# Five networks, five addresses for their rounded weights

## The chip, the cores and the metric

The kernel runs on one core of a Trainium2 chip. The metric is the time of one execution on the device in microseconds (us), the median of several runs. The profile is one further execution, recorded by the hardware profiler; its span goes from the first to the last instruction.

## The reference

Two transformer blocks are computed on 256 positions of width 1024, all in float32. In outline:

```
h = x;  h = h + mixer(rms_norm(h)) @ w_out
h = h + swiglu(rms_norm(h), w_gate, w_up, w_down)        # network 0; then rms_norm
for layer in 0, 1:
    x = x + 0.5 * swiglu(rms_norm(x), ffn_w_in[layer, 0], ffn_w_out[layer, 0])   # networks 1 and 3
    x = x + mixer_layer(rms_norm(x))
    x = x + 0.5 * swiglu(rms_norm(x), ffn_w_in[layer, 1], ffn_w_out[layer, 1])   # networks 2 and 4
swiglu(u) = (silu(u @ w_gate) * (u @ w_up)) @ w_down     # 1024 -> 2816 -> 1024
```

There are five such feed-forward networks ("ffn"), all of one size. Three mixers (attention of several kinds and two recurrences) lie between them, each with a projection in and one out.

## The kernel before

All weights come in through a ring of four slots of 128 x 3072 float32, loaded by SyncE's queue in the order of use. A network is worked off in 22 chunks of 128 of its 2816 inner columns; one chunk fills one slot: 1024 columns of gate, 1024 of up, 1024 of down.

The matrix products are done in a rounded float32 type (fp32r) that TensorE takes in one pass, and precision is regained by splitting each operand into a rounded part and the rounded rest. Each product is three passes, `PASSES = [(0, 0), (1, 0), (0, 1)]`: rounded weights by rounded activations, rest of the weights by rounded activations, rounded weights by the rest of the activations. For each chunk of a network

- ScalarE rounds gate and up into `w_gu[:, j, 0]` (`hi_a`, 2048 columns) and down into `w_dn[:, j, 0]` (`hi_b`, 1024 columns), where j is the chunk's parity;
- VectorE subtracts and leaves the rest in `w_gu[:, j, 1]` (`lo_a`) and `w_dn[:, j, 1]` (`lo_b`);
- TensorE does gate and up (`gate_up`): for each of 2 matrices, 8 pieces k and 3 passes, it loads 128 columns of `w_gu` as the stationary operand (a weight load, PEld) and streams 256 columns of the activations `uT_h` or `uT_l` past them (a matmul): 48 matmuls of 256 columns;
- ScalarE and VectorE make silu(gate) * up from the result and split it into `h_r`;
- TensorE does down (`down`) of the chunk before: here the activations `h_r` are stationary, 128 columns each, and 512 columns of `w_dn` are streamed: 12 matmuls of 512 columns.

TensorE loads the stationary operand of the next matmul while the present one streams. In a name such as `ps<-uT_h,w_gu` the streamed operand stands first, the stationary second, and in `ps<-w_dn,h_r` it is `w_dn` that is streamed.

The middle 16 chunks are a loop on each engine, the other six are written out; addresses repeat with the parity. The projections outside the networks use the same three passes with other buffers: `in_h`, `even_h`, `odd_h` for the rounded weights, `out_h` for those of the projections out, and `ring_r`, the ring itself, for the rest of their weights. Small sets of columns have `gate_w` (24 columns) and `odd_small` (8 columns).

Where things lie matters here, so the addresses are worked out from the sizes. Tensors are laid one after another. `x`, `xn`, `uT`, `yT` (whose space `uT_l` uses), `inh` (`in_h`), `gate_r`, `ring` and `ffb` (`h_r`) all have sizes that are multiples of 256 bytes, so all of them begin at the same address modulo 256. Then comes `cst` with 4662 float32, 18,648 bytes, which takes 18,656 with the next tensor at a multiple of 32; that is 224 modulo 256. `msk` (2304 bytes) and `small` (1024) keep it. So `wk`, the large work area that holds `w_gu`, `w_dn`, `even_h`, `odd_h` and `out_h`, begins 224 bytes past the activations modulo 256. Called phase below: (address of the weights minus address of the activations) modulo 256. Pieces within a tensor are 512 bytes apart for 128 columns and 1024 for 256, so the phase is the same for every matmul of a network: 224. In `in_h` and `ring_r` it is 0; in `even_h` and `out_h` it is 224. The slices of `gate_w` are 96 bytes apart and those of `odd_small` 32, so they go through many phases.

Of the kernel before, what the change touches and what calls it, by code (L numbers as in the profile page):

```python
# [7 lines left out]
F32 = mybir.dt.float32  # L8
# [7 lines left out]
P = 128  # L16
T, D = 256, 1024
TT, KC = T // P, D // P
F = 2816
FC = F // P  # L20
# [31 lines left out]


MASKS = 512 + 2 * LEVELS * P


IN_ITEMS = ([("col", 0), ("col", 1)] + [("col", b) for b in range(2, 6)] + [("zw", j) for j in range(4)]
# [38 lines left out]
def build(nc, x_in, wstream, gains, consts_in, masks_in, scratch, tri, inv, out):  # L96
    ctx = ExitStack()
    with ctx:
# [6 lines left out]
        def over(name, shape, under, skip=0):  # L105

            return nc.alloc_sbuf_tensor_at(name, shape, F32R, offset=at[under] + 4 * skip)
# [12 lines left out]
        s = {n: ctx.enter_context(nc.semaphore(n)) for n in names}  # L120
# [10 lines left out]
        cst = sb("cst", [P, NCONST])  # L131
        msk = sb("msk", [P, MASKS], U8)
        small = sb("small", [P, 256])
        WK = 20480
        wk = sb("wk", [P, WK])
        ps = [ctx.enter_context(nc.psum_tensor(f"ps{i}", [P, 512], F32)) for i in range(8)]
# [13 lines left out]

        ident = C("ident")

        w_gu = over("w_gu", [P, 2, 2, 2 * D], "wk")
        w_dn = over("w_dn", [P, 2, 2, D], "wk", 8 * D)
        h_r = over("h_r", [P, 2, 2, T], "ffb")
        ring_r = over("ring_r", [P, RING, SLOT], "ring")

# [5 lines left out]
        w_small = [over(f"even_small{i}", [P, KC * 40], "wk", 14336 + KC * 40 * i) for i in range(2)]  # L163
        wo_h = [over(f"out_h{i}", [P, SLOT], "wk", o) for i, o in enumerate((13312, 17408, 10240))]
        uT_r = [over("uT_h", [P, KC, T], "uT"), over("uT_l", [P, KC, T], "yT")]
        sg = wk[:, 12 * D:12 * D + 2 * T].rearrange("p (a b) -> p a b", a=2)
        ss = [small[:, 0:1], small[:, 1:2], small[:, 8:9]]
        ss3 = [small[:, 242:243], small[:, 243:244]]
        ss4 = [small[:, c:c + 1] for c in (0, 245, 1, 8)]
# [48 lines left out]
        mu_rest, k_a_rest = small[:, 224:238], small[:, 238:242]  # L218
        spread_heads = W(10240 + MASKS, P)

# [17 lines left out]
        MT_AT, n = {}, 0  # L238
# [140 lines left out]
        IB, n = {}, 0  # L379
# [51 lines left out]
        def _(sp):  # L431
# [3 lines left out]
            for i in range(RING):  # L435
# [5 lines left out]
                if i == 1:  # L441
                    sp.dma_start(cst[:, FIRST:NCONST], consts_in[:, FIRST:NCONST]).then_inc(s["consts_loaded"], 16)
            sp.dma_start(W(10240, MASKS + P), masks_in).then_inc(s["masks_loaded"], 16)
            rounds = (NSLOTS - RING) // RING
# [43 lines left out]
        def slot(i):  # L488
            return ring[:, i % RING, :]
# [3 lines left out]
        def _(pe):  # L493
# [3 lines left out]
            def mm(o, l, r, start=True, stop=True):  # L497
                return pe.matmul(o, l, r, start=start, stop=stop, skip_group_check=True)  # L498
# [49 lines left out]

            PASSES = [(0, 0), (1, 0), (0, 1)]

            def gate_up(j, between=None):
                for m in range(2):
                    if m and between:
                        between()
                    for k in range(KC):
                        for n, (a, b) in enumerate(PASSES):
                            w = w_gu[:, j % 2, a, (m * KC + k) * P:(m * KC + k + 1) * P]
                            last = mm(ps[4 + 2 * m + j % 2][:, 0:T], w, uT_r[b][:, k, :],
                                      k == 0 and n == 0, k == KC - 1 and n == 2)
                    last.then_inc(s[("gu_gate", "gu_ps")[m]], 1)  # L560

            def first_gate_up(norm):

                for k in range(KC):
                    pe.wait_ge(s["uT_hi"], 16 * TN[norm] + 8 + k + 1)
                    for m in range(2):
                        for a in range(2):
                            mm(ps[4 + 2 * m][:, 0:T], w_gu[:, 0, a, (m * KC + k) * P:(m * KC + k + 1) * P],
                               uT_r[0][:, k, :], k == 0 and a == 0, False)
                for m in range(2):  # L570
                    for k in range(KC):
                        if not m:
                            pe.wait_ge(s["uT_lo"], 16 * TN[norm] + 8 + k + 1)
                        last = mm(ps[4 + 2 * m][:, 0:T], w_gu[:, 0, 0, (m * KC + k) * P:(m * KC + k + 1) * P],
                                  uT_r[1][:, k, :], False, k == KC - 1)
                    last.then_inc(s[("gu_gate", "gu_ps")[m]], 1)

            def spread_rstd(norm):

                pe.wait_ge(s["diag_ready"], 2 * TN[norm] + 2)  # L580
                for t in range(TT):
                    last = mm(ps[0][:, t * P:(t + 1) * P], C("ones"), diag[:, t, :])
                last.then_inc(s["bc_ps"], 1)
                if norm == 1:
                    mm(ps[1][0:16, 0:384], C("t5")[0:32, :], C("t5_onehot")[0:32, :]).then_inc(s["t5_ps"], 1)

            def down_part(j, t, half, start, stop):
                for n, (a, b) in enumerate(PASSES):
                    last = mm(ps[2 * t + half][:, :], h_r[:, j % 2, a, t * P:(t + 1) * P],
                              w_dn[:, j % 2, b, half * 512:(half + 1) * 512], start and n == 0, stop and n == 2)  # L590
                return last

            def down(j, start):
                for t, half in PARTS:
                    last = down_part(j, t, half, start, False)
                last.then_inc(s["down_done"], 1)

            def ffn(f, norm):
                q = FC * f

                def step(c, r=0):

                    pe.wait_ge(s["lo_a"], r + (q + c + 1))
                    if q + c >= 2:
                        pe.wait_ge(s["h_ready"], r + (q + c - 1))
                    if c == 0:
                        first_gate_up(norm)
                    else:
                        gate_up(c, (lambda: spread_rstd(norm)) if c == 1 else None)
                    if 0 < c < FC - 1:  # L610
                        pe.wait_ge(s["lo_b"], r + (q + c))
                        pe.wait_ge(s["h_ready"], r + (q + c))
                        if norm == 1 and c == 1:
                            pe.wait_ge(s["t5_sb"], 1)
                        down(c - 1, c == 1)
                step(0)
                step(1)
                with pe.Fori(0, 4 * LOOPS, 4) as r:
                    for j in range(4):
                        step(2 + j, r)  # L620
                for c in range(2 + 4 * LOOPS, FC):
                    step(c)

                n = NORM_AFTER_FFN[f]
                pe.wait_ge(s["lo_b"], q + FC - 1)
                pe.wait_ge(s["h_ready"], q + FC - 1)
                for t, half in PARTS[0:3]:
                    down_part(FC - 2, t, half, False, False)
                pe.wait_ge(s["lo_b"], q + FC)
                pe.wait_ge(s["h_ready"], q + FC)  # L630
                for t, half in PARTS[0:3]:
                    down_part(FC - 1, t, half, False, True).then_inc(s["acc_done"], 1)
                first_T(n, 0)
                down_part(FC - 2, 1, 1, False, False).then_inc(s["down_done"], 1)
                down_part(FC - 1, 1, 1, False, True).then_inc(s["down_done"], 1)
                first_T(n, 1)

            def piece(o, j):
# [647 lines left out]
        def _(act):  # L1286
# [75 lines left out]
            def hi_a(f, c, r=0, rr=0):  # L1362

                q, i = FC * f, BASE[f"ffn{f}"] + c
                act.wait_ge(s[f"land{i % RING}"], rr + 16 * (i // RING + 1))
                if q + c >= 2:
                    act.wait_ge(s["gu_ps"], r + (q + c - 1))
                act.copy(w_gu[:, c % 2, 0, :], slot(i)[:, 0:2 * D]).then_inc(s["hi_a"], 1)  # L1368

            def hi_b(f, c, r=0):  # L1370
                q, i = FC * f, BASE[f"ffn{f}"] + c
                if q + c >= 2:
                    act.wait_ge(s["down_done"], r + (q + c - 1))
                act.copy(w_dn[:, c % 2, 0, :], slot(i)[:, 2 * D:3 * D]).then_inc(s["hi_b"], 1)  # L1374

            def ffn(f, norm):
                q = FC * f
# [585 lines left out]
        def _(v):  # L1963
# [60 lines left out]
            def lo_a(f, c, r=0):  # L2024

                q, i = FC * f, BASE[f"ffn{f}"] + c
                v.wait_ge(s["hi_a"], r + (q + c + 1))
                v.tensor_tensor(w_gu[:, c % 2, 1, :], slot(i)[:, 0:2 * D], w_gu[:, c % 2, 0, :].bitcast(F32),  # L2028
                                ALU.subtract).then_inc(s["lo_a"], 1)

            def lo_b(f, c, r=0):
                q, i = FC * f, BASE[f"ffn{f}"] + c
                v.wait_ge(s["hi_b"], r + (q + c + 1))
                v.tensor_tensor(w_dn[:, c % 2, 1, :], slot(i)[:, 2 * D:3 * D], w_dn[:, c % 2, 0, :].bitcast(F32),  # L2034
                                ALU.subtract).then_inc(s["lo_b"], 1)
                v.wait_ge(s["lo_b"], r + (q + c + 1))
                v.sem_inc(s[f"free{i % RING}"], 1)
# [762 lines left out]
```

## Time and profile before

| | |
|---|---|
| time, median of 3 runs | 1424.88 us (1424.19 to 1425.08) |
| span of the profiled execution | 1422.4 us |
| what lies around the span (median less span) | 2.5 us |
| TensorE matmul busy | 1395.2 us, 98% |
| VectorE busy | 944.7 us, 66% |
| ScalarE busy | 691.0 us, 49% |
| mean granted TensorE clock | 0.999 |

The profile gives the span only of the profiled execution, not a time of its own on the scale of the runs, so the difference between the median and the span stands in the table in its place. The busy time of one matmul in the profile contains its way through the array (some 0.28 us for 256 columns) and overlaps with the next one's. What a matmul costs in a row of many is the distance from one start to the next, and that is read from the timeline: take the starts of two rows and divide by the number of matmuls between them.

### The profile page before, as it was taken

The numbers are of one execution on the slowest core, as the hardware profiler recorded it, in microseconds if no ns is written. First come the engines' busy times: TensorE is split into PE (matmuls) and PEld (weight loads), VectorE is DVE, ScalarE is ACT, GpSimd is POOL, SyncE is SP. The second block draws the span as 40 slices with busy tenths as digits, with TensorE's granted clock in tenths as the row PEclk, the third lists the DMA queues.
The fourth block names the chain that finished last, engine by engine and source line by source line (L and its number), as shares of the span: only waits on it lengthen the run. The fifth ranks groups of instructions, "written<-read, shape, count | busy, mean of one in ns | idle before, by whom it ended". The sixth has DMA issues, their size and how long they took to land. (4 is left out here: it accounts for less than half of the span.)

```text
span 1422.4 us, 25483 instructions
## 1 busy us (share of the span) xinstructions
PE 1395.2 (98%) x10044; PEld 1286.2 (90%) x10044; DVE 944.7 (66%) x1539; ACT 691.0 (49%) x1107; POOL 82.9 (6%) x137
## 2 busy tenths in 40 slices
PE   8999999999999999999999999999999999999997
PEld 8898888999989999899989999999998988899997
DVE  5778567766668666567577666676665676676665
ACT  6764545433454443376654433444433655643342
POOL 1030010000020000000000000100000123000000
PEclk9999999999999999999999999999999999999999
DMA  9344005645526555433356545365554423465540
GB/s 359 135 160 185 2 25 228 222 177 183 197 108 228 209 184 177 178 104 133 120 207 224 189 177 182 129 229 198 194 177 178 149 90 134 177 222 180 194 158 30
DMA packets 33069, 239.47 MB, mean 168 GB/s; under 512 B 6864, under 2 KB 13280, under 8 KB 14304
## 3 DMA queue, kind: packets, MB, share of 16 engines
q1 hardware_dynamic: 30320, 234.84, 45.6%
q10 hardware_dynamic: 2672, 3.58, 0.7%
q8 instruction: 51, 0.84, 0.2%
q14 instruction: 26, 0.21, 0.0%
HBM read 236.15 MB, written 2.25 MB: 168 GB/s over the span
## 5 line engine op out<-in xcount | busy, mean ns | idle before, releaser
L498 PE MATMUL ps<-uT_h,w_gu 128*128 128x256 f32 x3520 | 614.1, 279 | 2.5 <-ACT uT_h L1316 2.5
L498 PEld LDWEIGHTS ps<-uT_h,w_gu 128*128 128x128 f32 x3520 | 538.0, 188 | 13.8 <-issue 5.0
L498 PE MATMUL ps<-uT_l,w_gu 128*128 128x256 f32 x1760 | 478.8, 279 | 0.0
L498 PE MATMUL ps<-w_dn,h_r 128*128 128x512 f32 x1320 | 325.7, 396 | 0.3 <-DVE h_r L2070 0.3
L498 PEld LDWEIGHTS ps<-uT_l,w_gu 128*128 128x128 f32 x1760 | 325.5, 188 | 0.0
L498 PEld LDWEIGHTS ps<-w_dn,h_r 128*128 128x128 f32 x1320 | 239.6, 188 | 51.3 <-issue 1.4
L1368 ACT CAST w_gu<-ring 128x2048 fp32r<-128x2048 f32 x110 | 210.0, 1909 | 156.2 <-PE ps L498 155.6
L2028 DVE TENSOR_TENSOR w_gu<-ring,w_gu 128x2048 fp32r<-128x2048 f32 x110 | 252.1, 2292 | 35.2 <-ACT w_gu L1368 35.2
L2061 DVE TENSOR_TENSOR us<-ps,bc 128x256 f32<-128x256 f32 x110 | 46.5, 423 | 203.2 <-PE ps L498 203.2
L1381 ACT ACTIVATE wk<-wk 128x256 f32<-128x256 f32 x110 | 46.1, 419 | 260.7 <-DVE wk L2059 260.7
L1374 ACT CAST w_dn<-ring 128x1024 fp32r<-128x1024 f32 x110 | 115.7, 1052 | 82.8 <-PE ps L498 82.7
L2034 DVE TENSOR_TENSOR w_dn<-ring,w_dn 128x1024 fp32r<-128x1024 f32 x110 | 134.1, 1219 | 5.3 <-ACT w_dn L1374 5.1
L498 PE MATMUL ps<-uT_h,ring_r 128*128 128x256 f32 x408 | 114.4, 281 | 0.0
L498 PE MATMUL ps<-wk 128*128 128x64 f32 (+6 forms) x504 | 76.9, 303 | 1.9 <-DVE small L2337 0.7
L498 PEld LDWEIGHTS ps<-uT_h,ring_r 128*128 128x128 f32 x408 | 77.5, 190 | 0.6 <-issue 0.2
L2059 DVE TENSOR_TENSOR wk<-ps,bc 128x256 f32<-128x256 f32 x110 | 46.7, 425 | 35.8 <-PE ps L498 22.0
L498 PEld LDWEIGHTS ps<-wk 128*128 128x128 f32 (+3 forms) x504 | 56.1, 186 | 7.4 <-issue 2.0
L498 PE MATMUL ps<-ring_r,uT_h 128*128 128x512 f32 (+2 forms) x176 | 62.0, 353 | 0.0
L2064 DVE TENSOR_TENSOR wk<-wk,us 128x256 f32<-128x256 f32 x110 | 46.7, 425 | 7.7 <-ACT wk L1381 4.3
L498 PE MATMUL ps<-uT_h,in_h 128*128 128x256 f32 x176 | 50.5, 289 | 1.0 <-DVE ring_r L2021 1.0
L2070 DVE TENSOR_TENSOR h_r<-wk,h_r 128x256 fp32r<-128x256 f32 x110 | 46.8, 425 | 3.7
L498 PE MATMUL ps<-uT_l,in_h 128*128 128x256 f32 x176 | 48.7, 283 | 0.0
(398 smaller groups left out, 1696.0 us busy)
## 6 DMA issues: line engine op xcount, KB each, us to landing
ring<-wstream SPq DMA_DIRECT2D x144, 1536.0 KB, 6.6
cst<-consts_in SPq DMA_DIRECT2D x1, 2185.0 KB, 13.7
wk<-t_row ACTq DMA_DIRECT2D x1, 2048.0 KB, 8.0
wk<-masks_in SPq DMA_DIRECT2D x1, 1216.0 KB, 24.1
x<-x_in SPq DMA_DIRECT2D x2, 512.0 KB, 4.7
ring<-wstream SPq DMA_DIRECT2D x1, 1024.0 KB, 8.8
inh<-gains ACTq DMA_DIRECT2D x2, 512.0 KB, 9.6
tri_blocks<-wk SPq DMA_DIRECT2D x3, 256.0 KB, 2.8
```

Of the source, the lines that this page charges most:

```text
L498: return pe.matmul(o, l, r, start=start, stop=stop, skip_group_check=True)
L1368: act.copy(w_gu[:, c % 2, 0, :], slot(i)[:, 0:2 * D]).then_inc(s["hi_a"], 1)
L1374: act.copy(w_dn[:, c % 2, 0, :], slot(i)[:, 2 * D:3 * D]).then_inc(s["hi_b"], 1)
L1381: act.activation(sg[:, c % 2, :], sg[:, c % 2, :], ACT.Silu).then_inc(s["silu_ready"], 1)
L2028: v.tensor_tensor(w_gu[:, c % 2, 1, :], slot(i)[:, 0:2 * D], w_gu[:, c % 2, 0, :].bitcast(F32), ALU.subtract).then_inc(s["lo_a"], 1)
L2034: v.tensor_tensor(w_dn[:, c % 2, 1, :], slot(i)[:, 2 * D:3 * D], w_dn[:, c % 2, 0, :].bitcast(F32), ALU.subtract).then_inc(s["lo_b"], 1)
L2059: v.tensor_tensor(h, ps[4 + c % 2][:, 0:T], bc[:], ALU.mult).then_inc(s["gs_ready"], 1)
L2061: v.tensor_tensor(us[:], ps[6 + c % 2][:, 0:T], bc[:], ALU.mult).then_inc(s["us_ready"], 1)
L2064: v.tensor_tensor(h, h, us[:], ALU.mult).then_inc(s["h_mul"], 1)
L2070: v.tensor_tensor(hr[:, 1, :], h, hr[:, 0, :].bitcast(F32), ALU.subtract).then_inc(s["h_ready"], 1)
```

## The change

`w_gu` and `w_dn`, one tensor each for all networks, become separate tensors for each network and parity. Network f begins FFN_AT[f] elements into `wk`, which is 64, 128, 192, 224 and 96 bytes; with the 224 of `wk` the phases are 32, 96, 160, 192 and 64. The buffers of the two parities are set apart by P = 128 elements (512 bytes), so that two networks' buffers of different parity do not overlap where one network's first chunks are rounded while the last one is being finished. `sg`, which holds the gate's result, moves 2048 bytes on. Nothing else changes: each instruction is there as before, in its order, with its waits.

```
+FFN_AT = [16, 32, 48, 56, 24]
...
-        w_gu = over("w_gu", [P, 2, 2, 2 * D], "wk")
-        w_dn = over("w_dn", [P, 2, 2, D], "wk", 8 * D)
+        w_gu = [[over(f"w_gu{2 * f + j}", [P, 2, 2 * D], "wk", FFN_AT[f] + j * (4 * D + P)) for j in range(2)]
+                for f in range(5)]
+        w_dn = [[over(f"w_dn{2 * f + j}", [P, 2, D], "wk", FFN_AT[f] + 2 * (4 * D + P) + j * (2 * D + P))
+                 for j in range(2)] for f in range(5)]
...
-        sg = wk[:, 12 * D:12 * D + 2 * T].rearrange("p (a b) -> p a b", a=2)
+        sg = wk[:, 12 * D + 4 * P:12 * D + 4 * P + 2 * T].rearrange("p (a b) -> p a b", a=2)
...
-                            w = w_gu[:, j % 2, a, (m * KC + k) * P:(m * KC + k + 1) * P]
+                            w = w_gu[f][j % 2][:, a, (m * KC + k) * P:(m * KC + k + 1) * P]
...
-                              w_dn[:, j % 2, b, half * 512:(half + 1) * 512], start and n == 0, stop and n == 2)
+                              w_dn[f][j % 2][:, b, half * 512:(half + 1) * 512], start and n == 0, stop and n == 2)
...
-                act.copy(w_gu[:, c % 2, 0, :], slot(i)[:, 0:2 * D]).then_inc(s["hi_a"], 1)
+                act.copy(w_gu[f][c % 2][:, 0, :], slot(i)[:, 0:2 * D]).then_inc(s["hi_a"], 1)
...
-                v.tensor_tensor(w_gu[:, c % 2, 1, :], slot(i)[:, 0:2 * D], w_gu[:, c % 2, 0, :].bitcast(F32),
+                v.tensor_tensor(w_gu[f][c % 2][:, 1, :], slot(i)[:, 0:2 * D], w_gu[f][c % 2][:, 0, :].bitcast(F32),
                                 ALU.subtract).then_inc(s["lo_a"], 1)
```

`hi_b`, `lo_b` and `first_gate_up` are changed in the same way.

## Rows read from the trace of the kernel before

**Rows 1.** The page: busy time, share and instructions; TensorE's clock in 40 slices
```profile
PE 1395.2 (98%) x10044; PEld 1286.2 (90%) x10044; DVE 944.7 (66%) x1539; ACT 691.0 (49%) x1107; POOL 82.9 (6%) x137
...
PEclk9999999999999999999999999999999999999999
```

**Rows 2.** Windows over networks 0 and 1, 2 and 3, and 4
```profile
226.00:601.80 375.80, 374.11 (x2666) 348.26 (x2666) 251.49 (x353) 161.35 (x177) 11.82 (x17) 1.00 0.54 194
726.60:1100.30 373.70, 373.15 (x2664) 348.09 (x2664) 247.97 (x347) 157.50 (x170) 5.48 (x9) 1.00 0.54 192
1229.20:1414.60 185.40, 185.40 (x1323) 173.17 (x1324) 120.39 (x170) 76.45 (x79) 1.49 (x4) 1.00 0.45 166
```

**Rows 3.** Groups on the page: forms, count, busy us, mean ns, idle before
```profile
L498 PE MATMUL ps<-uT_h,w_gu 128*128 128x256 f32 x3520 | 614.1, 279 | 2.5 <-ACT uT_h L1316 2.5
...
L498 PE MATMUL ps<-uT_l,w_gu 128*128 128x256 f32 x1760 | 478.8, 279 | 0.0
L498 PE MATMUL ps<-w_dn,h_r 128*128 128x512 f32 x1320 | 325.7, 396 | 0.3 <-DVE h_r L2070 0.3
```

**Rows 4.** Timeline, PE, network 0: two chunks in the loop
```profile
325.55 0.40 PE L498 MATMUL ps<-uT_h,w_gu 128*128 128x256 f32 x2
...
331.15 2.96 PE L498 MATMUL ps<-w_dn,h_r 128*128 128x512 f32 x12
333.95 0.40 PE L498 MATMUL ps<-uT_h,w_gu 128*128 128x256 f32 x2
```

**Rows 5.** Timeline, PE, projection in: phase 0; 12 matmuls between the first two rows
```profile
25.06 0.28 PE L498 MATMUL ps<-uT_h,ring_r 128*128 128x256 f32 x1
...
26.50 0.28 PE L498 MATMUL ps<-uT_h,ring_r 128*128 128x256 f32 x1
...
31.90 0.28 PE L498 MATMUL ps<-uT_h,ring_r 128*128 128x256 f32 x1
```

**Rows 6.** Timeline, PE, even projection, weights stationary: 54 matmuls between
```profile
614.22 0.28 PE L498 MATMUL ps<-uT_h,even_h 128*128 128x256 f32 x1
...
620.58 0.28 PE L498 MATMUL ps<-uT_h,even_h 128*128 128x256 f32 x1
```

**Rows 7.** Timeline, PE, even projection, weights streamed: 30 matmuls between
```profile
624.66 0.28 PE L498 MATMUL ps<-even_h,uT_h 128*128 128x256 f32 x1
...
628.19 0.28 PE L498 MATMUL ps<-even_h,uT_h 128*128 128x256 f32 x1
```

**Rows 8.** Timeline, PE, projection out, 512 columns streamed: 21 matmuls between
```profile
214.75 0.39 PE L498 MATMUL ps<-ring_r,uT_h 128*128 128x512 f32 x1
...
219.65 0.39 PE L498 MATMUL ps<-ring_r,uT_h 128*128 128x512 f32 x1
```

**Rows 9.** Timeline, PE, 24 stationary columns at many phases: 18 matmuls between
```profile
91.98 0.39 PE L498 MATMUL ps<-uT_h,gate_w 128*24 128x256 f32 x2
...
94.03 0.40 PE L498 MATMUL ps<-uT_h,gate_w 128*24 128x256 f32 x2
```

**Rows 10.** Timeline, PE, 8 stationary columns at many phases: 18 matmuls between
```profile
1109.23 0.39 PE L498 MATMUL ps<-uT_h,odd_small 128*8 128x256 f32 x2
...
1111.33 0.39 PE L498 MATMUL ps<-uT_h,odd_small 128*8 128x256 f32 x2
```

**Rows 11.** Groups, ACT and DVE, by form: rounding and subtracting at two phases
```profile
L1374 ACT CAST w_dn<-ring 128x1024 fp32r<-128x1024 f32 x110 | 115.7, 1052 | 82.8 <-PE ps L498 82.7
...
L1354 ACT CAST in_h<-ring 128x1024 fp32r<-128x1024 f32 x24 | 25.2, 1059 | 0.9 <-DMA ring<-wstream 0.3
...
L2034 DVE TENSOR_TENSOR w_dn<-ring,w_dn 128x1024 fp32r<-128x1024 f32 x110 | 134.1, 1219 | 5.3 <-ACT w_dn L1374 5.1
...
L2021 DVE TENSOR_TENSOR ring_r<-ring,in_h 128x1024 fp32r<-128x1024 f32 x24 | 31.0, 1296 | 12.2 <-ACT in_h L1354 11.5 <-DVE wk L2109 0.5
```

**Rows 12.** Timeline, DVE, network 0: the work of one chunk
```profile
331.35 0.42 DVE L2061 TENSOR_TENSOR us<-ps,bc 128x256 f32<-128x256 f32 x1 [2.37 <-PE ps L498]
...
332.59 0.42 DVE L2070 TENSOR_TENSOR h_r<-wk,h_r 128x256 fp32r<-128x256 f32 x1
333.35 2.29 DVE L2028 TENSOR_TENSOR w_gu<-ring,w_gu 128x2048 fp32r<-128x2048 f32 x1 [0.33 <-ACT w_gu L1368]
```

More of the change, by code:

```diff
@@ L549, in _, with gate_up @@
             PASSES = [(0, 0), (1, 0), (0, 1)]
-            def gate_up(j, between=None):
+            def gate_up(f, j, between=None):
                 for m in range(2):
@@ L560, in gate_up, with first_gate_up @@
                     last.then_inc(s[("gu_gate", "gu_ps")[m]], 1)
-            def first_gate_up(norm):
+            def first_gate_up(f, norm):
                 for k in range(KC):
@@ L567, in first_gate_up @@
                         for a in range(2):
-                            mm(ps[4 + 2 * m][:, 0:T], w_gu[:, 0, a, (m * KC + k) * P:(m * KC + k + 1) * P],
+                            mm(ps[4 + 2 * m][:, 0:T], w_gu[f][0][:, a, (m * KC + k) * P:(m * KC + k + 1) * P],
                                uT_r[0][:, k, :], k == 0 and a == 0, False)
@@ L573, in first_gate_up @@
                             pe.wait_ge(s["uT_lo"], 16 * TN[norm] + 8 + k + 1)
-                        last = mm(ps[4 + 2 * m][:, 0:T], w_gu[:, 0, 0, (m * KC + k) * P:(m * KC + k + 1) * P],
+                        last = mm(ps[4 + 2 * m][:, 0:T], w_gu[f][0][:, 0, (m * KC + k) * P:(m * KC + k + 1) * P],
                                   uT_r[1][:, k, :], False, k == KC - 1)
@@ L585, in spread_rstd, with down_part, down @@
                     mm(ps[1][0:16, 0:384], C("t5")[0:32, :], C("t5_onehot")[0:32, :]).then_inc(s["t5_ps"], 1)
-            def down_part(j, t, half, start, stop):
+            def down_part(f, j, t, half, start, stop):
                 for n, (a, b) in enumerate(PASSES):
                     last = mm(ps[2 * t + half][:, :], h_r[:, j % 2, a, t * P:(t + 1) * P],
-                              w_dn[:, j % 2, b, half * 512:(half + 1) * 512], start and n == 0, stop and n == 2)
+                              w_dn[f][j % 2][:, b, half * 512:(half + 1) * 512], start and n == 0, stop and n == 2)
                 return last
-            def down(j, start):
+            def down(f, j, start):
                 for t, half in PARTS:
-                    last = down_part(j, t, half, start, False)
+                    last = down_part(f, j, t, half, start, False)
                 last.then_inc(s["down_done"], 1)
@@ L606, in step @@
                     if c == 0:
-                        first_gate_up(norm)
+                        first_gate_up(f, norm)
                     else:
-                        gate_up(c, (lambda: spread_rstd(norm)) if c == 1 else None)
+                        gate_up(f, c, (lambda: spread_rstd(norm)) if c == 1 else None)
                     if 0 < c < FC - 1:
@@ L614, in step @@
                             pe.wait_ge(s["t5_sb"], 1)
-                        down(c - 1, c == 1)
+                        down(f, c - 1, c == 1)
                 step(0)
@@ L627, in ffn @@
                 for t, half in PARTS[0:3]:
-                    down_part(FC - 2, t, half, False, False)
+                    down_part(f, FC - 2, t, half, False, False)
                 pe.wait_ge(s["lo_b"], q + FC)
@@ L631, in ffn @@
                 for t, half in PARTS[0:3]:
-                    down_part(FC - 1, t, half, False, True).then_inc(s["acc_done"], 1)
+                    down_part(f, FC - 1, t, half, False, True).then_inc(s["acc_done"], 1)
                 first_T(n, 0)
-                down_part(FC - 2, 1, 1, False, False).then_inc(s["down_done"], 1)
-                down_part(FC - 1, 1, 1, False, True).then_inc(s["down_done"], 1)
+                down_part(f, FC - 2, 1, 1, False, False).then_inc(s["down_done"], 1)
+                down_part(f, FC - 1, 1, 1, False, True).then_inc(s["down_done"], 1)
                 first_T(n, 1)
@@ L1373, in hi_b @@
                     act.wait_ge(s["down_done"], r + (q + c - 1))
-                act.copy(w_dn[:, c % 2, 0, :], slot(i)[:, 2 * D:3 * D]).then_inc(s["hi_b"], 1)
+                act.copy(w_dn[f][c % 2][:, 0, :], slot(i)[:, 2 * D:3 * D]).then_inc(s["hi_b"], 1)
             def ffn(f, norm):
@@ L2033, in lo_b @@
                 v.wait_ge(s["hi_b"], r + (q + c + 1))
-                v.tensor_tensor(w_dn[:, c % 2, 1, :], slot(i)[:, 2 * D:3 * D], w_dn[:, c % 2, 0, :].bitcast(F32),
+                v.tensor_tensor(w_dn[f][c % 2][:, 1, :], slot(i)[:, 2 * D:3 * D], w_dn[f][c % 2][:, 0, :].bitcast(F32),
                                 ALU.subtract).then_inc(s["lo_b"], 1)
```

## The prediction

> **What bounds the kernel.** I read the page first: TensorE is busy 98% of the span at full clock, VectorE 66%, ScalarE 49% [rows 1]. The reader is to see that only TensorE can set the time. Then the windows over the five networks: they last 375.8, 373.7 and 185.4 us, 934.9 of 1422.4 us together, with TensorE busy in 932.7 of them and the granted clock 1.00, its upper level of 2.4 GHz [rows 2]. TensorE waits there for almost nothing: 2.5 and 0.3 us in front of the network's matmuls in all [rows 3]. So the networks cost what their matmuls cost, one after another, and the question is only whether an address changes that.
>
> The mean of one matmul (279 and 396 ns) [rows 3] does not tell, as it contains the way through the array. The starts do. In network 0 a chunk's 48 matmuls of gate and up go from 325.55 to 331.15, 5.60 us, and its 12 of down from there to 333.95, 2.80 us [rows 4]. That is 116.7 ns for 256 streamed columns and 233.3 ns for 512. The bare streaming at 2.4 GHz would be 106.7 and 213.3, so both pay the same 9.4% on top: proportional to the streamed columns, although the 512 have one weight load beside them like the 256. The whole is 5 x 22 x 8.4 = 924 us, which agrees with the windows less their beginnings and ends.
>
> **Does the address matter to TensorE?** The other stages show three things.
> - Where weights and activations have phase 0 throughout, in the projection in, the distance is 120.0 ns: 12 matmuls in 1.44 us, 57 in 6.84 [rows 5]. There every matmul costs 3.3 ns more than in the networks at phase 224, at the same clock.
> - In the even projection two of three operands of the weights lie at 224 and one, `ring_r`, at 0. With the weights stationary 54 matmuls take 6.36 us, 117.8 ns [rows 6]. If the third at phase 0 costs 120.0, the other two cost (3 x 117.8 - 120.0) / 2 = 116.7, the networks' value. Some part of the price goes with the address.
> - With the roles turned (weights streamed, activations stationary) the same mixture takes 3.53 us for 30, 117.7 ns [rows 7]. There the stationary operand lies 224 behind, which is 32 ahead, of the streamed one. So 32 costs what 224 costs, 116.7.
>
> With 512 streamed columns the mixture takes 4.90 us for 21, 233.3 ns [rows 8], exactly down's value: there a third at phase 0 costs nothing that can be seen.
>
> Small stationary operands go through many phases: 24 columns at steps of 96 bytes take 2.05 us for 18, 114 ns [rows 9], and 8 columns at steps of 32 bytes 2.10 us for 18, 116.7 ns [rows 10]. So the least seen is 114, the most 120, and 116.7 comes again and again, in the last case whatever the phase.
>
> **The Trainium skill on this.** The rows say that phase 0 costs 3.3 ns a matmul [rows 4, 5]. The Trainium skill, SBUF — State Buffer, section "Who interferes with whom", gives TensorE two independent read ports, one for the streamed operand and one for the weight load, and counts no contention between them; by it no phase could matter and the change would be worth exactly nothing. The trace does not agree for phase 0. The Trainium skill, TensorE: Matmul & The Clock Gate, section "Back-to-back issue gap", gives N / 2.4 + 2.5 ns, that is 109.2 for 256 and 215.8 for 512; if the new addresses brought that, 5280 x 7.5 + 1320 x 17.5 ns, an estimate of 63 us from that page, would go. No row of 256 or 512 columns in this rounded type reaches it.
>
> **The change part by part.**
> - Network 0, phase 32: 116.7 as before, by the turned mixture. 0 us. Down then has 224 as its own difference, which gate and up have now: 0.
> - Networks 1 and 2, phases 96 and 160, and networks 3 and 4, phases 192 and 64. No row shows 128 stationary columns at these. The bounds for a matmul of 256 are 113.9 and 120.0 [rows 9, 5]. There are 1056 in a network: 1056 x 2.8 = 3.0 us less at one end, 1056 x 3.3 = 3.5 us more at the other. For down (264 matmuls) the rows show no difference between a mixture and the phase 32 alone; in proportion to the columns its bounds are 264 x 5.6 = 1.5 less and 264 x 6.7 = 1.8 more. A network can move by -4.5 to +5.3 us, four of them by -18 to +21.
> - I take 0 for each of them, 116.7 ns. The nearest rows are those of 128 stationary columns at 224 and 32, and the 8 columns, which keep 116.7 through all multiples of 32.
> - Writing the weights: ScalarE's rounding takes 1052 ns at 224 and 1059 at 0; VectorE's subtraction 1219 against 1296, with another layout of the columns too [rows 11]. If all phases cost VectorE 6% on its 2292 and 1219 ns, that is 0.21 us per chunk. It is covered: `h_r` is ready at 332.59 + 0.42 = 333.01 and wanted by the down after the next gate and up, at 333.95 + 5.60 = 339.55; `w_gu` of the chunk after next is ready at 333.35 + 2.29 = 335.64 and wanted at 333.95 + 8.40 = 342.35 [rows 12, 4]. VectorE is busy 251.5 of 375.8 us in the networks 0 and 1 [rows 2]. Without that cover it would be 23 us for 110 chunks.
> - Buffers further apart, `sg` moved by 2048 bytes: no wait is added, nothing is moved past a queue, DMAs are the same. 0.
>
> Sum: 0 on 1422.4 us of span; with the 2.5 around it 1424.9. The median stands exactly there.
>
> **The rivals.**
> 1. *Collisions repeat every 64 bytes* (slower). If the two streams disturb one another when they meet in the same 64 bytes, then 64 and 192 are like 0, and 32, 96, 160 and 224 are one class. For it: 32 and 224 alike; and in the 8 columns the same times come back with every second piece. Against it: the 24 columns meet multiples of 64 as well and stay at 114 in the mean. Networks 3 and 4 then pay 2 x 3.5 = +7.0 us, 2 x 1.8 more if down pays too: 1432 to 1435.5. It decides once either is over 117.0 ns a matmul with nothing gained elsewhere.
> 2. *Distance helps* (faster). 0 costs most, 32 less, and further away it goes on falling to the 114 seen. For it: 120, 116.7 and 114 are all there. Against it: 8 columns at many phases stay at 116.7. With 64 and 192 alone at 114 it is 2 x 3.0 = 6 us, with all four and down 18: 1419 to 1407.
> 3. *Other phases are worse* in a way that no row shows, beyond the class of 64: two or four networks at 120 or so, +7 to +21: 1432 to 1446.
> 4. *The address is not the cause*: the projection in is slow for its banks or its code, and nothing changes. Same time as my forecast, and no network differs from another; I count it with it.
>
> **How the numbers follow.** A measurement of this kernel tells about 0.2%, 2.85 us, from no change: less than one network at either bound. No network moves, or they cancel (with rival 4): 0.40. Rival 1: 0.18. Rival 3: 0.12, with a part of 0.01 that cancels. Rival 2: 0.30. So faster 0.29, as its smallest forms stay within 0.2%; same 0.40; slower 0.31, with small mixed cases. The forecast is 1424.9, by itself from 1423 to 1427. The range takes the middle of rival 2 and rivals 1 and 3 without their ends: 1411 to 1438.
>
> **What the next profile would show.** The same two rows of the timeline in each network: a chunk's 48 matmuls in 5.60 us and its 12 in 2.80. Rival 1: 5.76 in networks 3 and 4 alone, and 5.60 in 1 and 2. Rival 2: 5.5 or less in some. Network 0 must keep 5.60 in every case; if not, the reading of the mixtures was wrong and with it the symmetry between the operands. Gate and up could move and down not; that would say that the weight load, of which both have one per matmul, matters less beside the longer stream. Casts and subtractions stay at 1.05 and 1.22 us within 1%. I would be wrong above all if phases have an effect of another size than the 3.3 ns of phase 0, since I know 128 stationary columns at only three phases out of eight.

## The result and the profile after

The changed kernel takes 1427.88 us in the median of 9 runs (1426.8 to 1433.57), the kernel before 1424.66 (1423.92 to 1425.08, 9 runs). The ratio is 1.0026 with a 95% interval of 1.0017 to 1.0035: 3.2 us or 0.26% slower, a little more than the 0.2% (2.85 us) that the prediction took as the least a measurement can tell from no change, and with the lower end of the interval inside it. Eight of the nine runs lie between 1426.8 and 1428.3 us; why one took 1433.57 no trace shows. The profiled execution has a span of 1426.5 us against 1422.4.

The page of the changed kernel, busy time and clock, beside [rows 1]:
```profile
PE 1399.8 (98%) x10044; PEld 1291.9 (91%) x10044; DVE 945.2 (66%) x1539; ACT 689.9 (48%) x1107; POOL 82.8 (6%) x137
...
PEclk9999999999999999999999999999999999999999
```
TensorE has the same number of instructions, the full clock, and 4.6 us more.

The windows of the changed kernel over networks 0 to 4, one each (columns as in [rows 2]: stretch, length, busy us and counts of PE, PEld, DVE, ACT, POOL, clock, DMA share, GB/s):
```profile
226.49:414.72 188.23, 188.23 (x1329) 175.36 (x1330) 122.69 (x171) 80.78 (x85) 3.35 (x6) 1.00 0.56 203
417.13:605.78 188.65, 187.77 (x1323) 175.43 (x1324) 127.08 (x177) 78.58 (x87) 6.20 (x10) 1.00 0.51 184
730.81:919.65 188.84, 188.84 (x1328) 176.80 (x1329) 122.48 (x170) 78.74 (x82) 1.48 (x4) 1.00 0.54 197
922.06:1108.22 186.16, 186.16 (x1324) 173.87 (x1324) 123.70 (x172) 76.62 (x83) 3.99 (x5) 1.00 0.52 186
1237.12:1418.79 181.67, 181.67 (x1324) 170.49 (x1324) 120.30 (x170) 76.20 (x79) 1.48 (x4) 1.00 0.47 170
```
The same windows of the kernel before last 186.54, 186.84, 185.84, 185.39 and 185.43 us, 930.0 in all. So the networks changed by +1.7, +1.8, +3.0, +0.8 and -3.8 us, together +3.5 of the span's +4.1. The small result is a sum of two larger parts of opposite sign.

The timeline of the changed kernel, PE, one chunk in the loop of networks 0, 2 and 4, beside [rows 4]:
```profile
309.97 0.40 PE L503 MATMUL ps<-uT_h,w_gu 128*128 128x256 f32 x2
...
315.64 2.96 PE L503 MATMUL ps<-w_dn,h_r 128*128 128x512 f32 x12
318.44 0.40 PE L503 MATMUL ps<-uT_h,w_gu 128*128 128x256 f32 x2
...
814.14 0.40 PE L503 MATMUL ps<-uT_h,w_gu 128*128 128x256 f32 x2
...
819.89 2.96 PE L503 MATMUL ps<-w_dn,h_r 128*128 128x512 f32 x12
822.68 0.40 PE L503 MATMUL ps<-uT_h,w_gu 128*128 128x256 f32 x2
...
1317.65 0.40 PE L503 MATMUL ps<-uT_h,w_gu 128*128 128x256 f32 x2
...
1323.12 2.91 PE L503 MATMUL ps<-w_dn,h_r 128*128 128x512 f32 x12
1325.87 0.40 PE L503 MATMUL ps<-uT_h,w_gu 128*128 128x256 f32 x2
```
The distance from the first row to the second is gate and up (48 matmuls), from the second to the third down (12): 5.67 and 2.80 us in network 0, 5.75 and 2.79 in network 2, 5.47 and 2.75 in network 4. Before it was 5.60 and 2.80 in each.

From here on, chunk times are medians over the chunks of a network, taken in this way from the starts in the trace, to the nanosecond. They repeat to some 10 ns from chunk to chunk, apart from the first ones of a network. The "per matmul" columns are these times divided by 48 and by 12. Kernels are called by their labels below (all64 is e1_all64, and so on). In us per chunk, for all networks in which gate and up and down have the same phase and the loads are as in the change:

| phase, gate and up and down alike | gate and up | per matmul | down | per matmul | kernels |
|---|---|---|---|---|---|
| 224 | 5.600 | 116.7 ns | 2.800 | 233.3 ns | before, five networks; screen and split, network 3 |
| 32 | 5.682 | 118.4 | 2.797 | 233.1 | after, network 0; permuted, network 1 |
| 96 | 5.698 | 118.7 | 2.795 | 232.9 | after, network 1 |
| 96 | 5.633 | 117.4 | 2.814 | 234.5 | permuted, network 2 |
| 160 | 5.746 | 119.7 | 2.794 | 232.8 | after, network 2; permuted, network 3 |
| 192 | 5.650 | 117.7 | 2.803 | 233.6 | after, network 3; permuted, network 4 (5.653, 2.800) |
| 64 | 5.466 | 113.9 | 2.748 | 229.0 | after, network 4; all64, five networks; permuted, network 0; screen and split, network 2; projections, the other four |
| 64 | 5.653 | 117.8 | 2.767 | 230.6 | projections, network 2 |
| 0 | 5.753 | 119.9 | 2.747 | 228.9 | screen, network 0; split, network 4 (5.752, 2.748) |
| 128 | 5.698 | 118.7 | 2.776 | 231.3 | screen, network 1 |

Two phases stand in it twice, with two times. That is what the later experiments are about.

### The profile page after: what moved, and what is told of

Its sections match the earlier page's. It is cut to its first block and busy times, and to the rows that moved or that the text cites. A ratio compares the mean times of both kernels' runs of the same rounds, so it can differ in the third digit from the quotient of the medians.

```text
span 1426.5 us, 25483 instructions
## 1 busy us (share of the span) xinstructions
PE 1399.8 (98%) x10044; PEld 1291.9 (91%) x10044; DVE 945.2 (66%) x1539; ACT 689.9 (48%) x1107; POOL 82.8 (6%) x137
## 5 line engine op out<-in xcount | busy, mean ns | idle before, releaser
L1373 ACT CAST w_gu<-ring 128x2048 fp32r<-128x2048 f32 x110 | 209.4, 1904 | 158.5 <-PE ps L503 157.5
L2033 DVE TENSOR_TENSOR w_gu<-ring,w_gu 128x2048 fp32r<-128x2048 f32 x110 | 252.2, 2292 | 34.6 <-ACT w_gu L1373 34.6
L1379 ACT CAST w_dn<-ring 128x1024 fp32r<-128x1024 f32 x110 | 115.4, 1049 | 82.1 <-PE ps L503 82.0
L2039 DVE TENSOR_TENSOR w_dn<-ring,w_dn 128x1024 fp32r<-128x1024 f32 x110 | 134.1, 1219 | 5.2 <-ACT w_dn L1379 5.0
```

Source lines behind the costliest of these rows:

```text
L1373: act.copy(w_gu[f][c % 2][:, 0, :], slot(i)[:, 0:2 * D]).then_inc(s["hi_a"], 1)
L1379: act.copy(w_dn[f][c % 2][:, 0, :], slot(i)[:, 2 * D:3 * D]).then_inc(s["hi_b"], 1)
L2033: v.tensor_tensor(w_gu[f][c % 2][:, 1, :], slot(i)[:, 0:2 * D], w_gu[f][c % 2][:, 0, :].bitcast(F32), ALU.subtract).then_inc(s["lo_a"], 1)
L2039: v.tensor_tensor(w_dn[f][c % 2][:, 1, :], slot(i)[:, 2 * D:3 * D], w_dn[f][c % 2][:, 0, :].bitcast(F32), ALU.subtract).then_inc(s["lo_b"], 1)
```

## Experiments

### Is it the phase or the network: all at 64, the phases permuted, the missing phases

All at 64 (label e1_all64):
```
-FFN_AT = [16, 32, 48, 56, 24]
+FFN_AT = [24, 24, 24, 24, 24]
```


> All five networks have the phase of network 4 of the changed kernel, 64. Theory A (what counts is the distance of stationary and streamed operand modulo 256, and nothing else of a network): each chunk costs what it cost in network 4 of the changed kernel, 5.466 us for gate and up and 2.748 for down, 8.214 against 8.400 before, so 110 x 0.186 = 20.5 us less than the kernel before: about 1404. Rival C (it is the network and what surrounds it, not the phase): networks 0 to 3 keep the 8.45 to 8.54 us per chunk that they have in the changed kernel, about 1428.

Measured: 1407.35 us in the median of 4 runs (1404.70 to 1409.41), ratio to before 0.9881 (0.9863 to 0.9899). The timeline of this kernel, PE, a chunk of network 0:
```profile
307.41 0.40 PE L503 MATMUL ps<-uT_h,w_gu 128*128 128x256 f32 x2
...
312.87 2.91 PE L503 MATMUL ps<-w_dn,h_r 128*128 128x512 f32 x12
315.62 0.40 PE L503 MATMUL ps<-uT_h,w_gu 128*128 128x256 f32 x2
```
5.46 and 2.75 us, where network 0 had 5.67 and 2.80 in the changed kernel. All five networks have 5.466 and 2.748, so the time goes with the phase and rival C falls. The four runs lie in two groups, 1404.7 and 1405.6, 1409.1 and 1409.4. The projections kernel below suggests a reason, which is not shown for this kernel.

The same five phases in another order (label e2_permuted):
```
-FFN_AT = [16, 32, 48, 56, 24]
+FFN_AT = [24, 16, 32, 48, 56]
```


> The five phases of the changed kernel in another order: 64, 32, 96, 160, 192 for networks 0 to 4. Theory A: the chunk times go with the phase, that is gate and up 5.47, 5.68, 5.70, 5.75, 5.65 us and down 2.75, 2.80, 2.80, 2.79, 2.80; the whole is that of the changed kernel, 1428. Rival C: the networks keep 5.68, 5.70, 5.75, 5.65, 5.47.

Measured: 1426.98 us, one run. Gate and up 5.466, 5.682, 5.633, 5.747, 5.653 us; down 2.748, 2.799, 2.814, 2.793, 2.800. Four of five are the value of their phase to within 3 ns. The third, phase 96 in network 2, has 5.633 where network 1 of the changed kernel had 5.698. What could explain it comes with the kernel of the moved activations.

The phases not in the change (label e3_screen):
```
-FFN_AT = [16, 32, 48, 56, 24]
+FFN_AT = [8, 40, 24, 0, 88]
```


> Phases 0, 128, 64, 224 for networks 0 to 3, and for network 4 a distance of 320 bytes, which is 64 modulo 256 but not modulo 512. Theory A: network 2 has 5.47 us of gate and up, network 3 has 5.60 with the buffers set apart as in the changed kernel, network 4 is like network 2 (5.47); network 0 has 5.76 by the 120.0 ns of the projection in; network 1 is unknown, between 5.47 and 5.76. Rival (the address counts modulo 512 or more): network 4 differs from 5.47. Rival (the gap of 512 bytes between the parities is what costs time): network 3 is over 5.64.

Measured: 1420.84 us, one run. The timeline of this kernel, PE, networks 0 and 4:
```profile
310.76 0.40 PE L503 MATMUL ps<-uT_h,w_gu 128*128 128x256 f32 x2
...
316.51 2.91 PE L503 MATMUL ps<-w_dn,h_r 128*128 128x512 f32 x12
319.26 0.40 PE L503 MATMUL ps<-uT_h,w_gu 128*128 128x256 f32 x2
...
1310.19 0.40 PE L503 MATMUL ps<-uT_h,w_gu 128*128 128x256 f32 x2
...
1315.66 2.91 PE L503 MATMUL ps<-w_dn,h_r 128*128 128x512 f32 x12
1318.41 0.40 PE L503 MATMUL ps<-uT_h,w_gu 128*128 128x256 f32 x2
```
At 0 gate and up take 5.75 us, the 120 ns of the projection in, and down 2.75, its quick value: what is worst for one is good for the other. At 320 bytes gate and up take 5.47, as at 64, so here 256 bytes more make no difference. Network 3, at 224 with the buffers set apart as in the change, has 5.600: the gap of 512 bytes between the parities costs nothing. The order is not one of distance: 64 is the best for gate and up, its neighbour 96 and 128 are among the bad, and 192, which is 64 on the other side, has 5.650 us.

### The difference or the weights' own address

The activations moved by 96 bytes (label e5_act96):
```
+        sb("pad0", [P, 24])
         uT = sb("uT", [P, KC, T])
         yT = sb("yT", [P, KC, T])
+        sb("pad1", [P, 40])
```


> The weights lie as in the changed kernel against all else, but the activations uT_h and uT_l are moved 96 bytes up, h_r is not. For gate and up the phases become 192, 0, 64, 96, 224 in networks 0 to 4; for down nothing changes. Theory A (difference): gate and up 5.65, 5.76, 5.47, 5.70, 5.60 us, down 2.80, 2.80, 2.79, 2.80, 2.75. Rival B (the weights' own address counts, not the difference): gate and up stay 5.68, 5.70, 5.75, 5.65, 5.47.

Measured: 1429.81 us, one run. Gate and up 5.657, 5.741, 5.653, 5.698, 5.606 us. Networks 0, 1, 3 and 4 have the values of the phases 192, 0, 96 and 224 to within 12 ns, and none keeps that of the weights' address: rival B falls. Network 4, with the weights where they were quick in the changed kernel, is back at 5.61; its down, whose own operands were not moved, goes from 2.748 to 2.768 beside it. But network 2, now at 64, has 5.653 instead of 5.47. The timeline of this kernel, PE, the third and fourth chunks of network 2:
```profile
745.41 0.41 PE L505 MATMUL ps<-uT_h,w_gu 128*128 128x256 f32 x2
...
750.88 2.96 PE L505 MATMUL ps<-w_dn,h_r 128*128 128x512 f32 x12
753.67 0.40 PE L505 MATMUL ps<-uT_h,w_gu 128*128 128x256 f32 x2
...
759.33 2.96 PE L505 MATMUL ps<-w_dn,h_r 128*128 128x512 f32 x12
```
The third chunk is quick, 750.88 - 745.41 = 5.47 us, and the fourth, with the same instructions on buffers laid out alike, takes 759.33 - 753.67 = 5.66, as do all that follow. No address differs between them modulo 256; what TensorE did just before does. From this came theory A2: at one phase there are several rhythms, stable once entered, and the entry decides.

### Several rhythms at one phase

Gate and up and down with phases of their own (label e4_split):
```
-FFN_AT = [16, 32, 48, 56, 24]
+FFN_AT = [24, 0, 24, 0, 8]
+DN_AT = [0, 24, 24, 0, 8]
...
-        w_dn = [[over(f"w_dn{2 * f + j}", [P, 2, D], "wk", FFN_AT[f] + 2 * (4 * D + P) + j * (2 * D + P))
+        w_dn = [[over(f"w_dn{2 * f + j}", [P, 2, D], "wk", DN_AT[f] + 2 * (4 * D + P) + j * (2 * D + P))
```


> Gate and up and down have phases of their own. Networks 0 to 4: gate and up 64, 224, 64, 224, 0; down 224, 64, 64, 224, 0. Theory A1 (the phase alone fixes the time, for gate and up and for down apart): gate and up 5.47, 5.60, 5.47, 5.60, 5.75 us; down 2.80, 2.75, 2.75, 2.80, 2.75. Theory A2 (at one phase TensorE can run in more than one rhythm, and what ran before picks it, as in the kernel with moved activations, where gate and up at 64 took 5.65 after a down at 160): network 0, whose down is at 224, has 5.6 or more for gate and up although its phase is 64.

Measured: 1424.61 us, one run. Gate and up 5.658, 5.604, 5.466, 5.600, 5.752 us; down 2.795, 2.764, 2.748, 2.800, 2.748. With gate and up at 64 and down at 224 (network 0) gate and up take 5.658; with both at 64 (network 2) 5.466. A1 falls. Down at 64 after gate and up at 224 has 2.764, a little above its 2.748.

Gate and up at 64, down at 0 in all networks (label e8_down0; `FFN_AT` all 24 and `DN_AT` all 8):

> Gate and up at 64, down at 0, in all networks. By the screen down takes 2.747 us at 0 and 2.748 at 64, so Theory A1 gives the same as with all at 64, 1404 to 1409. Theory A2: if down at 0 leads gate and up into the slow rhythm, gate and up take 5.65 us and the time is 110 x 0.18 = 20 us more, about 1425.

Measured: 1424.00 us in the median of 10 runs (1423.14 to 1424.30), ratio 0.9994 (0.9985 to 1.0004). Gate and up 5.653, down 2.746: the gain of all64 is gone although both phases are quick ones. In the profiles the networks are 3.3 to 3.6 us longer than all64's, 17.6 us in all; that is 0.187 us for each chunk of gate and up except the first ones of a network, which are quicker: 5.50 to 5.55 us in the third chunk of networks 1 to 4. A1 falls here too.

An extra matmul ahead of each chunk's gate and up in the same kernel (label e11_nudge):
```
             def gate_up(f, j, between=None):
+                if n := (0, 32, 64, 128, 192)[f]:
+                    mm(ps[4 + j % 2][:, T:T + n], w_gu[f][j % 2][:, 0, 0:P], uT_r[0][:, 0, 0:n])
```


> The kernel with gate and up at 64 and down at 0, which ran gate and up in 5.653 us, with one more matmul ahead of each chunk's gate and up, from the second chunk on, into an unused part of the bank: 0, 32, 64, 128, 192 streamed columns in networks 0 to 4. It adds nothing to the result. Theory A2: some of these shifts bring gate and up into the quick rhythm, 48 matmuls in 5.44 to 5.47 us and with the extra one 5.5 to 5.6; network 0 keeps 5.653. Rival A1 (the phases of gate and up and down fix the rhythm by themselves): 5.65 in all, plus the extra matmul, 5.7 to 5.75.

Measured: 1418.36 us, one run, some 6 us less than without the extra work. The timeline of this kernel, PE, networks 0 (none added) and 2 (64 columns, the first of the three matmuls in its first row):
```profile
309.37 0.40 PE L504 MATMUL ps<-uT_h,w_gu 128*128 128x256 f32 x2
...
315.02 2.91 PE L504 MATMUL ps<-w_dn,h_r 128*128 128x512 f32 x12
317.77 0.40 PE L504 MATMUL ps<-uT_h,w_gu 128*128 128x256 f32 x2
...
806.95 0.51 PE L504 MATMUL ps<-uT_h,w_gu 128*128 128x64 f32 x3
...
812.51 2.91 PE L504 MATMUL ps<-w_dn,h_r 128*128 128x512 f32 x12
815.25 0.51 PE L504 MATMUL ps<-uT_h,w_gu 128*128 128x64 f32 x3
```
Gate and up of network 0 take 5.65 us with 48 matmuls and of network 2 5.56 with 49. After the first two or three matmuls its distances are for the most part 113, 113 and 114 ns, against 117 to 119 in network 0. All four lengths did it: whole chunks of 8.400 us without, and 8.313, 8.307, 8.320 and 8.320 with. More work in less time, with no address of the 48 changed, shows that the rhythm is not fixed by the addresses alone.

### The projections too

All weights 64 bytes past the activations, `h_r` with them (label e6_everywhere):
```
-FFN_AT = [16, 32, 48, 56, 24]
+FFN_AT = [0, 0, 0, 0, 0]
...
+        sb("pad0", [P, 16])
         inh = sb("inh", [P, KC * 3 * P])
...
+        sb("pad1", [P, 8])
         wk = sb("wk", [P, WK])
```


> All buffers of weights, those of the projections too, lie 64 bytes past the activations, by 64 bytes left free after uT_l and 32 before wk; h_r is moved too, so down has 0. Theory A: networks as with all at 64 (5.466 and 2.747 us); the 1224 matmuls of 256 columns in the projections go from 120.0 or 117.8 to 113.9 ns, some 6 us, and the 288 of 512 columns from 233.3 to 229, 1.2 us: 7 us less than with the networks alone, 1397 to 1401. Rival (projections gain nothing, as they wait for other things): 1404 to 1408.

Measured: 1418.08 us in the median of 5 runs (1416.49 to 1419.37), ratio 0.9952 (0.9938 to 0.9965). The timeline of this kernel, PE, the projection in (60 matmuls from the first row to the second) and network 2, beside [rows 5, 4]:
```profile
25.15 0.28 PE L505 MATMUL ps<-uT_h,ring_r 128*128 128x256 f32 x1
...
31.95 0.28 PE L505 MATMUL ps<-uT_h,ring_r 128*128 128x256 f32 x1
...
806.20 0.40 PE L505 MATMUL ps<-uT_h,w_gu 128*128 128x256 f32 x2
...
811.86 2.88 PE L505 MATMUL ps<-w_dn,h_r 128*128 128x512 f32 x12
814.58 0.40 PE L505 MATMUL ps<-uT_h,w_gu 128*128 128x256 f32 x2
```
The projection in goes from 120.0 to 6.80 / 60 = 113.3 ns. Down goes to 2.72 us, 226.7 ns, less than at any phase before, although its two operands differ by 0 as in down0, where it took 2.746. But gate and up take 5.653, as in down0, whose phases of 64 and 0 this kernel shares. The expectation for the networks failed: gate and up stay in the slow rhythm, and of the gain only that of down and of the projections is left. That the projection in follows the address too, with its code and its PSUM banks as before, settles rival 4 of the prediction.

The same for the weights, but `h_r` left at the activations' phase, by laying `ffb` before the free 64 bytes (label e9_projections):

> As all64 for the networks (gate and up at 64, down at 64, h_r at the activations' own phase, for which ffb is laid before inh), and the weights of the projections at 64 too. Theory A2: the networks keep 5.466 and 2.748 us per chunk, because down runs as in all64; the projection in runs at 113.3 ns as it did in everywhere; the whole is 2 to 7 us less than all64, 1398 to 1404. Rival (h_r's or w_dn's absolute address matters as well, which could also be why everywhere was slow): gate and up at 5.65, about 1420.

Measured: 1405.23 us in the median of 4 runs (1402.01 to 1407.31), ratio 0.9855 (0.9838 to 0.9871). The timeline of this kernel, PE, a chunk of networks 1 and 2:
```profile
492.22 0.40 PE L505 MATMUL ps<-uT_h,w_gu 128*128 128x256 f32 x2
...
497.69 2.91 PE L505 MATMUL ps<-w_dn,h_r 128*128 128x512 f32 x12
500.44 0.40 PE L505 MATMUL ps<-uT_h,w_gu 128*128 128x256 f32 x2
...
799.67 0.40 PE L505 MATMUL ps<-uT_h,w_gu 128*128 128x256 f32 x2
...
805.32 2.93 PE L505 MATMUL ps<-w_dn,h_r 128*128 128x512 f32 x12
808.09 0.40 PE L505 MATMUL ps<-uT_h,w_gu 128*128 128x256 f32 x2
```
Networks 0, 1, 3 and 4 have 5.466 and 2.748 us; network 2, with the same code and the same phases, has 5.653 and 2.767 in every chunk from the fourth on, 186.24 us in the window against 182.1 in all64's. So within one execution one network falls into one rhythm and another into the other. The third chunk does not tell them apart: it takes 5.71 us in networks 2, 3 and 4, and only network 2 goes on slowly. One network in the slow rhythm costs 20 x 0.206 = 4.1 us. That is near the distance of 1402.0 from 1406.4 and 1407.3 here and of the two groups of all64, but the fourth run here, 1404.07, lies in the middle, and only the run of 1407.31 has a trace: that the spread of the runs comes from such networks is not shown.

The projections gained less than forecast. The time outside the five networks (from the first to the last start of a network's matmuls) is 490.0 us here and 490.3 in everywhere, 492.6 in all64 and 492.1 to 494.0 in all the other kernels: some 2 to 3 us against all64, where 7 were expected in everywhere.

All64 once more, to see this in it (label e10_all64_again, no edit against all64):

> The same kernel as all64, whose four runs fell into two groups, 1405 and 1409. Theory A2: one or more networks or chunks have another rhythm in the slower group, so this profile shows either 5.466 and 2.748 everywhere (1405) or one network with more (1409). Rival: the slower runs have the same chunks and lose the 4 us outside the networks or all over, by the clock.

Measured: 1406.87 us, one run, all five networks at 5.466 and 2.748. It has not caught a slow network, and it lies between the groups, not at the 1405 expected for five quick networks. For all64 the account of the two groups is carried over from the projections kernel and not shown. Of the 1.3 us between its span and the first run's (1405.1 and 1403.8) 1.1 lie ahead of network 0, which starts at 227.19 against 226.13 us.

Taken over all kernels, the phase of down decides almost always how gate and up at 64 run. With down at 64 too, 19 of 20 networks are in the quick rhythm, network 2 above being the other. With down at 0, 160 or 224 and nothing added between, none of 13 is: all of down0 and everywhere, network 0 of nudge and of split, network 2 of act96.

### Who is the partner of the stream

One column instead of 128 in the weight load of `gate_up` (label e7_one_column); what the networks compute is another thing for that:
```
-                            w = w_gu[f][j % 2][:, a, (m * KC + k) * P:(m * KC + k + 1) * P]
+                            w = w_gu[f][j % 2][:, a, (m * KC + k) * P:(m * KC + k) * P + 1].to_broadcast([P, P])
```


> The kernel with five phases, but after a network's first chunk gate_up takes one column of the piece of weights 128 times instead of 128 columns, so the weight load reads one place over and over. What the networks compute is another thing for that; count and shape of the instructions are the same. Theory D (two walks through the memory meet: the weight load's and the stream's): without the weight load's walk the phases cost alike, one value for gate and up in all networks but for 32-byte classes, while down keeps 2.80, 2.80, 2.79, 2.80, 2.75. Rival (the start address alone sets the rhythm): 5.68, 5.70, 5.75, 5.65, 5.47 as before.

Measured: 1411.74 us, one run. The timeline of this kernel, PE, network 2, to be held against network 2 of the changed kernel above:
```profile
805.11 0.39 PE L503 MATMUL ps<-uT_h,w_gu 128*128 128x256 f32 x2
...
810.55 2.97 PE L503 MATMUL ps<-w_dn,h_r 128*128 128x512 f32 x12
813.36 0.39 PE L503 MATMUL ps<-uT_h,w_gu 128*128 128x256 f32 x2
```
Gate and up 5.611, 5.458, 5.443, 5.451, 5.462 us against 5.682, 5.698, 5.746, 5.650, 5.466 with 128 columns read. The instructions and their number are the same; only where the weight load reads has changed, and 4 of 5 networks now lie within 20 ns of one another, 113.4 to 113.8 ns a matmul. After the first matmuls of a chunk all four run at 113.3 ns, the distance of the quick rhythm at 64, and a weight load has 188 ns in the profile before and after, so it has not become shorter. So most of what these phases cost in gate and up goes away when the weight load no longer walks through its 512 bytes beside the stream's 1024. Whether the walk itself costs the time, or only keeps the row out of the quick rhythm, this run does not tell apart. That phase 32 stays at 116.9 ns was not expected: with the walk gone there is still a dependence on the start. Down, whose loads are untouched, has 2.80, 2.81, 2.81, 2.80 and 2.75, within 17 ns of the changed kernel.

The Trainium skill, SBUF — State Buffer, section "Who interferes with whom", was weighed in the prediction: two independent read ports, no contention. The measurements decide against it as far as time goes. With the ports as they are, the same loads beside the same streams take from 113.9 to 119.9 ns a matmul by address alone, and in four networks of five gate and up lose most of the excess when the load stays in one place. How the two meet inside the memory is not shown by any run.

## Why the prediction was right or wrong

**The bound and the place: right.** TensorE alone sets the time; the subtractions kept their 2292 and 1219 ns on VectorE and the casts 1904 and 1049 ns on ScalarE against 1909 and 1052, and TensorE waited for neither. What moved is the distance between matmuls, in the networks.

**The number: right within its range, but for a wrong reason.** 1424.9 was forecast, 1427.9 measured, inside 1411 to 1438 and outside the likeliest case's own 1423 to 1427. The likeliest case was that no network moves. Every network moved. The sum came out small because networks 0 to 3 lost 7.3 us and network 4 gained 3.8. A cancellation had been counted in the 0.40 beside the case of no movement, and had a hundredth in rival 3. That the total landed inside the range is luck: by the chunk times of the table, the same edit with all five at 64 or all at 160 would have moved it by -20 or +15 us, out of the range on either side.

**The step that failed** is the one for network 0: "So 32 costs what 224 costs, 116.7", from the even projection with the roles turned, and with it "Network 0 must keep 5.60 in every case". Network 0 went to 5.682 us. The step took it that in a mixture each matmul pays the price of its own phase, so that it can be solved for one of them, and that a row with stationary activations tells the price of one with stationary weights. With the prices measured later, (2 x 116.7 + 120.0) / 3 = 117.8 is what [rows 6] show, but (2 x 118.4 + 120.0) / 3 = 118.9 is not the 117.7 of [rows 7]. Which of the two assumptions fails there no run tells; against the first speaks that even one and the same phase has two prices (5.466 and 5.653). The symmetry between the operands that the prediction drew from this step is gone as well: 32 and 224 are mirror images and have 5.682 and 5.600, 64 and 192 have 5.466 and 5.650.

**The step for networks 1 to 4**, "I take 0 for each of them", from the 8 columns that keep 116.7 ns whatever their phase: also wrong, by +1.8, +3.0, +0.8 and -3.8 us. A load of 8 columns walks 32 bytes, one of 128 columns 512, and the kernel with one column shows that the extent of the walk matters, so the 8 columns were a poor neighbour of the 128. Loads of 8 columns were not tried further. The bounds held: 113.9 to 119.7 ns in the changed kernel within 113.9 to 120.0, and down 229.0 to 233.6 within 227.7 to 240.0. The least of down in any run, 226.7, is below.

**Down** was held not to move; it gained 0.05 us a chunk at 64 and 0, which is 1.1 us a network. The mixture of [rows 8], a third of it at phase 0, did not show it: it has 233.3 ns, where (2 x 233.3 + 228.9) / 3 = 231.9 would follow if each matmul paid the price of its own phase.

**The rivals.** Rival 1 (64 bytes): fallen, 64 is the best and 192 the least bad of the other four. Rival 2 (distance helps): fallen as a law, as 128 is bad, though its price was right for the one phase, 64. Rival 3 (other phases worse in a way no row shows) is what happened in networks 0 to 3, at the small end of its price: 7.3 us, and 117.7 to 119.7 ns a matmul in place of 120. Rival 4 (the address is not the cause): fallen, by the permutation, and for the projection in by everywhere.

**The formula for the gap.** N / 2.4 + 2.5 ns in the prediction, by the Trainium skill, TensorE: Matmul & The Clock Gate, section "Back-to-back issue gap", would be 109.2 ns. The page gives it for an isolated matmul and says that it counts too much at large N, which the prediction left out. The quickest rhythm in these kernels is 113.3 for 256 columns and 226.7 for 512, more than the formula's 109.2 and 215.8.

## What to carry to other kernels

Where TensorE runs without gaps, take the distance between starts, not the mean duration, and compare stages of the same shape: two stages with 120.0 and 116.7 ns at the same clock were the sign here that the address matters, and 1.2 to 1.5% of the time was won by it in the end. Place the stationary and the streamed operand of fp32r matmuls by trial, one phase per repeated stage of a single kernel, then all at the best: 64 bytes for both products gave 1407.35 us, and with the projections 1405.23 us (ratio 0.9855, 0.9838 to 0.9871), which is not apart from the former beyond the intervals, though the time outside the networks fell by 2 to 3 us in the traces. And measure the combination, since a phase that is quick beside one predecessor was slow beside another: 64 with 0 gave nothing at all.

## What was not expected of the hardware

- A row of matmuls settles into a repeating rhythm, and at one placement of the operands there can be two: 113.3 and 117.8 ns for 256 columns. Once the first few chunks of a network are past, the one entered lasts to its end, and it can differ between networks that are laid out alike in one execution.
- An added matmul of 64 columns ahead of 48 others shortened the chunk from 8.400 to 8.307 us.
- With 128 different stationary columns and 256 streamed, the distances in the networks average between 113.9 and 119.9 ns over a chunk, a span of 5%, with the granted clock at 1.00 in the windows over the networks.
- What stays open: the rule that gives the rhythm from the two addresses and the entry, why down takes 226.7 ns a matmul where its operands lie 64 bytes past the activations and 228.8 where both lie at 0, and whether finer steps than 32 bytes, in which tensors are placed here, would do better. None of these was tried.
